# A two-layer decoder trunk: rounded weights of 22 mixer pieces brought by casting transfers, a preset mask in all heads but the first, constants prepared later

## The reference

```python
def mixer(u, w_in, ret_gn, w_ret_proj, w_sb_proj, w_out, pos, valid):
    rq, rk, rv, rg, sq, sk, sv, ga, gb = jnp.split(u @ w_in, SPLITS, axis=-1)
    ...
    o_r = retention(rotary(heads(rq, 8), pos), rotary(heads(rk, 8), pos), heads(rv, 8), valid)
    ...                                              # normalise each head over its 128 values
    y_ret = (jax.nn.silu(rg) * (o_r * ret_gn)) @ w_ret_proj
    o_s = stick_breaking(heads(sq, 8), heads(sk, 8), heads(sv, 8), valid)
    y_sb = o_s @ w_sb_proj
    return (jax.nn.sigmoid(ga) * y_ret + jax.nn.sigmoid(gb) * y_sb) @ w_out

# stick breaking: z = q k / sqrt(d), causal mask, then
# a = exp(log_sigmoid(z) + sum over later keys of log_sigmoid(-z))
for l in range(DEPTH):
    h = h + 0.5 * swiglu(rmsnorm(h, ffn1_norm[l]), ffn1_w_gu[l], ffn1_w_down[l])
    h = h + mixer(rmsnorm(h, mix_norm[l]), ...)
    h = h + 0.5 * swiglu(rmsnorm(h, ffn2_norm[l]), ffn2_w_gu[l], ffn2_w_down[l])
```

## Time and profile before

| | |
|---|---|
| Median of 3 runs | 1290.34 us |
| The profiled execution | 1290.29 us, of which the span of instructions 1288.5 us |
| PE busy | 1280.2 us, 99% of the span |
| DVE, ACT, POOL busy | 867.1 us, 697.9 us, 54.4 us |
| Traffic | 219.30 MB, mean 170 GB/s |
| Granted TensorE clock | 0.999 of full speed |

### The profile page before, as it was taken

One profiled execution on the slowest core, in us unless ns is written; L12 is line 12 of the kernel. 1 busy time (PEld: TensorE's weight loads), 2 busy tenths in 40 slices (PEclk: granted clock), 3 DMA queues, 4 the chain that ended last, 5 costly groups with the idle time before them and its releaser, 6 DMA issues.

```text
span 1288.5 us, 26136 instructions
## 1 busy us (share of the span) xinstructions
PE 1280.2 (99%) x10302; PEld 1275.3 (99%) x10302; DVE 867.1 (67%) x1083; ACT 697.9 (54%) x937; POOL 54.4 (4%) x48
## 2 busy tenths in 40 slices
PE   9999999999999999999999999999999999999998
PEld 8999999999999999999999999999999999999998
DVE  7766546878776776665476665568788777766653
ACT  6544445757766554444454444457578665544442
POOL 2000001000000010000010000010000000100000
PEclk9999999999999999999999999999999999999999
DMA  7655554554344455555545555545443445655552
GB/s 293 200 179 176 179 170 159 183 167 142 120 143 143 159 188 179 166 179 180 173 157 193 175 170 177 179 165 180 168 144 131 140 157 179 197 185 183 186 180 82
DMA packets 60705, 219.30 MB, mean 170 GB/s; under 512 B 6864, under 2 KB 6992, under 8 KB 60496
## 3 DMA queue, kind: packets, MB, share of 16 engines
q1 hardware_dynamic: 60192, 217.27, 50.3%
q10 hardware_dynamic: 432, 0.85, 0.2%
HBM read 217.04 MB, written 1.05 MB: 169 GB/s over the span
## 4 chain that ended last, share of the span: by engine, by line
PE 98%; ACT 1%; DVE 1%; DMA 0%; DVEq 0%; issue 0%
PE bank L1122 31%; PE bank L1124 31%; PE bank L1123 31%; PE bank L1278 1%; PE bank L1370 1%; PE bank L1399 1%; PE bank L1267 1%; PE bank L1250 0%; DMA raw<-stream 0%; PE bank L1285 0%; ACT xh L414 0%; DVE w_lo L667 0%; ACT w_hi L409 0%; PE bank L1268 0%; PE bank L1377 0%; PE bank L1378 0%
## 5 line engine op out<-in xcount | busy, mean ns | idle before, releaser
L667 DVE TENSOR_TENSOR w_lo<-raw,w_hi 128x1024 fp32r<-128x1024 f32 x407 | 508.7, 1256 | 270.0 <-ACT w_hi L409 265.4
L1122 PE MATMUL bank<-xh,w_hi 128*128 128x272 f32 (+1 forms) x2224 | 641.5, 288 | 0.9 <-DVE w_lo L667 0.9
L409 ACT ACTIVATE w_hi<-raw 128x1024 fp32r<-128x1024 f32 x407 | 427.8, 1057 | 390.0 <-PE bank L1124 389.0
L1124 PE MATMUL bank<-xh,w_lo 128*128 128x272 f32 (+1 forms) x2224 | 635.8, 286 | 0.0
L1123 PE MATMUL bank<-xl,w_hi 128*128 128x272 f32 (+1 forms) x2224 | 635.6, 286 | 0.0
L1122 PEld LDWEIGHTS bank<-xh,w_hi 128*128 128x128 f32 x2224 | 418.3, 188 | 1.2 <-DVE w_lo L667 1.1
L1123 PEld LDWEIGHTS bank<-xl,w_hi 128*128 128x128 f32 x2224 | 418.6, 188 | 0.0
L1124 PEld LDWEIGHTS bank<-xh,w_lo 128*128 128x128 f32 x2224 | 418.0, 188 | 0.0
L1124 PE MATMUL bank<-gh,w_lo 128*128 128x272 f32 (+1 forms) x1016 | 290.9, 286 | 0.0
L1122 PE MATMUL bank<-gh,w_hi 128*128 128x272 f32 (+1 forms) x1016 | 290.6, 286 | 0.0
L1123 PE MATMUL bank<-gl,w_hi 128*128 128x272 f32 (+1 forms) x1016 | 289.7, 285 | 0.0
(11 more groups left out here) (203 smaller groups left out, 734.7 us busy)
## 6 DMA issues: line engine op xcount, KB each, us to landing
raw<-stream SPq DMA_DIRECT2D x407, 512.0 KB, 3.3
table<-tables SPq DMA_DIRECT2D x1, 1424.0 KB, 7.7
out<-rv_gb SPq DMA_DIRECT2D x3, 256.0 KB, 2.7
gain_h<-tokens SPq DMA_DIRECT2D x2, 272.0 KB, 6.1
raw<-stream SPq DMA_DIRECT2D x2, 256.0 KB, 4.3
rv_gb<-squares SPq DMA_DIRECT2D x1, 384.0 KB, 8.0
gain_h<-tokens ACTq DMA_DIRECT2D x1, 300.0 KB, 4.1
gain_h<-tokens ACTq DMA_DIRECT2D x1, 272.0 KB, 4.9
```

Of the source, the lines that this page charges most:

```text
L409: eng.activation(w_hi[:, slot, :], raw[:, slot, :], ACT.Copy).then_inc(hi_ready, 1)
L667: eng.tensor_tensor(w_lo[:, slot, :], raw[:, slot, :], w_hi[:, slot, :].bitcast(F32), ALU.subtract).then_inc(lo_ready, 1)
L1122: pe.matmul(out, wh, hi, start=first, stop=False)
L1124: mm = pe.matmul(out, wl, hi, start=False, stop=last)
```

## The change

Three parts.

1. In each layer, the 22 pieces whose rounding belongs to steps s = 24 to 45 of the mixer (`CAST`) are no longer rounded by ACT. POOL issues a DMA transfer from the weight stream to `w_hi`, whose type float32r differs from float32, so the transfer casts. It is issued when PE has finished piece s, the same moment that released ACT's rounding. The piece is still loaded to `raw` as well, and DVE's subtraction waits for both transfers. POOL's placing of keys and queries is divided into three functions, and two of them now stand between these transfers.
2. `KEPT_MASKS` goes from 3 to 1.
3. DVE's preparation of `square_r` and `z_mask` moves from the opening to behind the first block's hidden loop.

```diff
-KEPT_MASKS = 3
+KEPT_MASKS = 1
+CAST = range(24, 46)
 ...
+            def cast_hi(l, s):
+                n, slot = l * PER_LAYER + FFN + s + RING, (FFN + s) % RING
+                pool.wait_ge(piece_done, n - (RING - 1))
+                pool.dma_start(w_hi[:, slot, :], stream[n]).then_inc(hi_in[slot], 16)
+
+            def mixer(l):
+                place_first_keys(l)
+                for s in CAST:
+                    cast_hi(l, s)
+                    if s == 2 * U_SK + 4:
+                        place_second_keys(l)
+                    if s == 2 * U_SQ[1] + 1:
+                        place_last_queries(l)
 ...
-                    split_hi(base + (s + RING), (FFN + s) % RING)
+                    if s not in CAST:
+                        split_hi(base + (s + RING), (FFN + s) % RING)
 ...
+            def split_cast(l, s):
+                slot = (FFN + s) % RING
+                eng.wait_ge(hi_in[slot], 16 * cast_count(l, s))
+                eng.wait_ge(raw_ready[slot], (l * PER_LAYER + FFN + s + RING - slot) * (16 // RING) + 16)
+                remainder(slot)
 ...
+                if fi == 0:
+                    constants_in()
 ...
                     for n in [] if s == MIX - 2 else [s - 1, s] if s == MIX - 1 else [s]:
-                        split_lo(base + (n + RING), (FFN + n) % RING)
+                        if n in CAST:
+                            split_cast(l, n)
+                        else:
+                            split_lo(base + (n + RING), (FFN + n) % RING, casts_before(l, n))
 ...
             split_lo(3, 3)
-            eng.wait_ge(squares_in, 32)
-            eng.tensor_copy(square_r[:, 0:C_NEG], square[:, :]).then_inc(masks_ready, 1)
-            eng.tensor_copy(square_r[:, C_NEG:], staged).then_inc(masks_ready, 1)
-            eng.memset(z_mask[:, :], 0.0).then_inc(masks_ready, 1)
 ...
             layers(layer)
```

More of the change, by code:

```diff
@@ L247, in evicted, with casts_before, cast_count @@
             return l * UNITS + (u - U_V + 1)
+        def casts_before(l, s):
+            return l * len(CAST) + len([c for c in CAST if c < s])
+        def cast_count(l, s):
+            return len([c for c in CAST if c % RING == s % RING]) * l + len([c for c in CAST if c % RING == s % RING and c <= s])
         def layers(layer):
@@ L255, in trunk @@
         raw_ready = [sem(f"raw_ready{i}") for i in range(RING)]
+        hi_in = [sem(f"hi_in{i}") for i in range(RING)]
         hi_ready, lo_ready, piece_done = sem("hi_ready"), sem("lo_ready"), sem("piece_done")
@@ L357, in layer @@
                     if i == 2:
-                        place_queries(l)
+                        mixer(l)
                     for p in range(1, PAIRS):
@@ L372, in place_tail_queries, with place_first_keys @@
                 mm.then_inc(placed, 1)
-            def place_queries(l):
+            def cast_hi(l, s):
[10 more added lines that the diff above has]
+                        place_last_queries(l)
+            def place_first_keys(l):
                 pool.wait_ge(ssum_done, l * 3 + 2)
@@ L380, in place_queries, with place_second_keys @@
                 pool.wait_ge(rq_tail_in, l + 1)
+            def place_second_keys(l):
                 pool.wait_ge(ret_tail_scores, l + 1)
@@ L384, in place_queries, with place_last_queries @@
                 pool.wait_ge(key_tail_ready, 2 * l + 2)
+            def place_last_queries(l):
                 pool.wait_ge(unit_evicted, evicted(l, U_SQ[1]))
@@ L663, in _, with split_lo, remainder @@
         def _(eng):
-            def split_lo(n, slot):
-                eng.wait_ge(hi_ready, n + 1)
+            def split_lo(n, slot, casts=0):
+                eng.wait_ge(hi_ready, n + (1 - casts))
+                remainder(slot)
[3 more added lines that the diff above has]
+                eng.wait_ge(raw_ready[slot], (l * PER_LAYER + FFN + s + RING - slot) * (16 // RING) + 16)
+                remainder(slot)
+            def remainder(slot):
                 eng.tensor_tensor(w_lo[:, slot, :], raw[:, slot, :], w_hi[:, slot, :].bitcast(F32),
@@ L719, in last_pair, with constants_in @@
                     gain_of(rnd, c)
+            def constants_in():
+                eng.wait_ge(squares_in, 32)
+                eng.tensor_copy(square_r[:, 0:C_NEG], square[:, :]).then_inc(masks_ready, 1)
+                eng.tensor_copy(square_r[:, C_NEG:], staged).then_inc(masks_ready, 1)
+                eng.memset(z_mask[:, :], 0.0).then_inc(masks_ready, 1)
+                eng.wait_ge(masks_ready, 3)
+                for c in (0, T):
+                    mm = eng.tensor_copy(z_mask[:, c:c + P], staged[:, 0:P])
+                mm.then_inc(masks_ready, 1)
             def ffn(l, f):
@@ L725, in ffn @@
                 last = first_query(l) > 0 and f == 1
+                casts = casts_before(l + f, 0)
                 q0 = first_query(l) if f else 0
@@ L739, in next_lo @@
                 def next_lo(it, j):
-                    split_lo(base + it * 4 + (j + RING), (off + j) % RING)
+                    split_lo(base + it * 4 + (j + RING), (off + j) % RING, casts)
                 def hidden(it):
@@ L782, in ffn @@
                             if not last or n + RING < FFN:
-                                split_lo(base + (n + RING), (off + n) % RING)
+                                split_lo(base + (n + RING), (off + n) % RING, casts)
             def mixer(l):
```

## The result

| | before | after |
|---|---|---|
| Median, range | 1290.32 us (1290.28 to 1290.52, 4 runs) | 1369.83 us (1363.97 to 1375.65, 4 runs) |
| Ratio to before | | 1.0616 [1.0597, 1.0634] |
| Profiled execution, its span | 1290.29, 1288.5 us | 1375.65, 1373.8 us |
| Mean granted clock | 0.999 | 0.978 |

The change is slower by 79.5 us. Its four runs stand in pairs, 1364.0 and 1364.5 us at a granted clock of 0.987 to 0.989, and 1375.2 and 1375.7 us at 0.978.

The account below looks back on a forecast made before the run. PE was taken to bound the kernel, busy 1280.2 of 1288.5 us. 1290.29 us plus 63.3 for the casts, minus 0.64 for masks and 0.93 for the opening, gave 1352.0 us; range 1316 to 1416.

Parts of the forecast that it names:

- Slower, by DVE's wait: Steps 24 to 45: DVE waits for each transfer's landing, other heads' work queued behind, so PE idles; slower 0.95.
- 11 a layer: Places where PE waits for DVE's work behind a transfer: 8 for retention heads, 3 for stick-breaking heads, bearing 20.1 us.
- L: Time from a piece's end on PE to DVE's subtraction; taken as 3.3 + 1.4 = 4.7 us, forecast between 3.0 and 7.6.
- its own formula: Cost of the casting transfers over two layers, 22 L - 40.1 us; 63.3 us at the likeliest L of 4.7.
- 3 us each at full clock: Sign of being right: in steps 24 to 45 PE idles some 11 times a layer, some 3 us each, clock not falling.
- rival 2: PE's clock falls in the gaps; half of the 84.4 us stretch at half speed in each layer, 1436 us; chance 0.07.
- Traffic: In the stretch of steps 24 to 45, loads plus 11.5 MB of casts stay moderate, under 200 GB/s.
- rival 3: Casts and loads delay each other, or the cast is slow: L 7.6 to 9.0 us, 1416 to 1447 us; chance 0.06.
- Rival 1: Transfers are hidden, landing before the 11 places need them; not slower, 1288.7 us at L of 1.5; chance 0.05.
- ACT: 44 roundings of 1.06 us, 46.6 us, leave ACT; counted as nothing, since ACT is 1% of the chain.
- Constants: Moved from the opening, where PE waits 0.93 us: that wait goes; the new place costs nothing, at most 1.8 us.
- the cover: Four added mask presets of 0.52 us fall in steps that lose a 1.06 us rounding; otherwise at most 2.1 us.

Follow-up runs that it names:

- the version two steps later: The change with all three parts, but DVE makes each cast piece's remainder two steps after its transfer (last two in step 46): 1289.24 us, ratio 0.9991.

## Why the prediction was right, and where it wasn't

**Slower, by DVE's wait: right.** PE waits at 22 places, 16 for `dec` and 6 for the running sums, which is the prediction's 11 a layer, and but for one wait of 0.1 us nowhere else for the casts. Taking DVE's work from behind the wait removes the loss with all transfers in place; lengthening the wait raises it.

**L: mis-sized, 4.3 instead of 4.7.** The landing counts from the start of the issuing instruction, so POOL's part, 0.53 us, lies within it, and the prediction put 1.4 us for it on top of a landing. The landing itself is longer than its 3.3: 3.7 us at the median of all 44 and 4.28 on average at the 22 places. By its own formula the casts would cost 22 x 4.33 - 40.1 = 55.2 us of idle time at full clock; 55.6 were measured. So what the places bear was right in the sum, 22 waits of 2.5 us on average; single places were off by up to 0.7 us either way.

The Trainium skill ("DMA: Bandwidth & Descriptors", Anatomy of one DMA, SWDGE (gpsimd) path) has the fit from which the prediction worked out its estimate of 3.2 us. The trace differs: from the start of POOL's instruction the 44 transfers took 3.4 us at the least and 3.7 at the median.

**"3 us each at full clock": the step that failed.** The sum had no term for the clock and put it into rival 2, at 0.07. Part of that rival happened: the mean clock of the two stretches is 0.89 and 0.90, and PE's own work costs 30.6 us more in the profiled run, and some 20 in the two runs near 1364 if their waits are the same. The prediction had named a clock below 1.00 as a sign that it was wrong, and this sign came. The reason it gave against the clock's fall, that PE works for 3 to 7 us without a pause between gaps, wasn't enough: PE works for 9.2 us between the first two gaps, from 292.35 to 301.59, and the clock falls again at the second. But rival 2's price, half of the stretch at half speed or 84 us, was far too high, since the clock fell behind some gaps only and came back, in step 24 after 4 us. With L at 4.33 and the 30.6 us of the clock (the mask matmuls are already off it) the sum is 1290.29 + 55.2 - 0.93 + 30.6 = 1375.2 us, where the profiled run took 1375.65. The predicted 1352 came out 18 us low, and that it wasn't more is luck: the too large L covered 8 of some 26 us that were missing. The stretch of 84.4 us became 123 and not 116 for the same reason.

**Traffic: right.** Under 200 GB/s were predicted, 179 and 181 measured, so rival 3 (L of 7.6 to 9) didn't occur; the longest landing was 5.8 us. Rival 1 (hidden) is what the version two steps later does, and it came out 0.5 us above where that rival had put it: 1288.7 predicted, 1289.2 measured.

**ACT: right.** The 44 roundings are gone, 46.6 us by their group's total, and no time was gained. ACT's busy total fell by 39.3 us. Of the difference the presets explain some 2; most of the rest is overlap, since the total counts once the time in which two of ACT's instructions overlap, such as the rounding of step 45 before (369.99 to 371.05) and the instruction that starts at 370.96. Added up one by one, ACT's instructions fell by 43.9 us.

**Constants: right.** PE's wait at 19.92 is gone, and alone they gain 1.12 us. **Masks: the cover was rightly named.** Without it they cost 1.4 us (at most 2.1 was said); the 0.64 us that they should save can be seen in PE's busy total of the last kernel, 1279.6 us against 1280.3 with constants alone, but not in its time, which is no faster.

## What to carry to other kernels

A step handed to a transfer is free only if nothing that others need is queued behind the wait on the engine that takes its result: count the places where someone waits for that engine, ask how much delay each bears, and move the consumer by a step or two rather than the transfer. Where gaps of some microseconds come often into a stretch in which PE was never idle, add a term for the clock to the idle time, sized by rows and not by the whole stretch at half speed. Two waits on parallel paths to the same consumer don't add up: the later of them decides.

## What the hardware showed beyond that

The clock doesn't fall behind every gap, even of the same length. PE of after in order of time, behind a gap of 2.65 us and behind one of 2.66:

```profile
304.24 1.75 PE L1420 MATMUL bank<-dec,rv_gb 128*128 128x272 f32 x4 [2.65 <-DVE dec L1071]
...
306.01 0.43 PE L1173 MATMUL bank<-xl,w_hi 128*128 128x272 f32 x1
...
339.39 0.97 PE L1420 MATMUL bank<-dec,rv_gb 128*128 128x272 f32 x4 [2.66 <-DVE dec L1071]
...
340.33 0.29 PE L1173 MATMUL bank<-xl,w_hi 128*128 128x272 f32 x1
```

Behind the first the four products of `dec` take 1.75 us and a matmul of a piece 0.43, behind the second 0.97 and 0.29; the granted clock of the two cuts shown with the result, 0.77 from 300 us and 1.00 from 330, says the same. Nor does it always fall in the gap itself: in step 24 it fell only when PE had worked again for 0.9 us. Work in the gap keeps the clock: 0.998 with 2.4 us of useless matmuls at each place, 0.994 with half of that, 0.978 to 0.989 with none. The Trainium skill ("TensorE: Matmul & The Clock Gate", Part 1: The HAM clock gate) has the clock follow PE's activity, and these runs agree; why one gap costs the clock and another of the same length doesn't stays open.

The same work on DVE takes longer beside POOL's additions. In the opening of after, DVE and POOL in order of time:

```profile
11.56 1.22 DVE L708 TENSOR_TENSOR w_lo<-raw,w_hi 128x1024 fp32r<-128x1024 f32 x1
...
15.57 5.85 DVE L708 TENSOR_TENSOR w_lo<-raw,w_hi 128x1024 fp32r<-128x1024 f32 x3 [0.48 <-ACT w_hi L438]
```

```profile
14.15 4.47 POOL L363 TENSOR_TENSOR ssq<-ssq,xg 128x544 f32<-128x544 f32 x2
18.70 1.63 POOL L372 TENSOR_TENSOR ssq<-ssq 128x272 f32<-128x272 f32 x1
```

A subtraction takes 1.22 us before POOL's additions start and 1.95 on average from 15.57 on, when POOL adds until 20.33. The Trainium skill ("SBUF — State Buffer", Who interferes with whom) says that a DVE instruction with two SBUF inputs contends with a GpSimd instruction that reads SBUF; the rows agree with that, at 0.7 us a subtraction, though no run here changed this alone. The constants gain by their new place too, where POOL is at rest: 3.28 us in the opening before, and 146.14 - 144.54 = 1.60 here:

```profile
144.54 0.29 DVE L765 CAST square_r<-square 128x256 fp32r<-128x256 f32 x1
...
146.14 2.36 DVE L708 TENSOR_TENSOR w_lo<-raw,w_hi 128x1024 fp32r<-128x1024 f32 x2
```
